# A decoder trunk's MLP: from two token halves to two stages, with a seven-product up projection

## The chip, the cores and the metric
The kernel runs on one core of one Trainium2 chip. The metric is the device time of one execution in microseconds; lower is better. Runs agree to within about 0.3%.

## The reference
One layer of a hybrid decoder for T = 2080 tokens (2048 of a prompt, 32 of eight sample sequences) with model width D = 1024: RMSNorm, one combined projection, three groups of heads (window attention, dilated attention, an RWKV-7 recurrence), an output projection added to the residual, and then the part that is changed, all in float32:
```
x = x + mix @ w_out
u = rmsnorm(x, norm2_g) @ mlp_up            # 1024 -> 4096
x = x + square(relu(u)) @ mlp_down          # 4096 -> 1024
y = rmsnorm(x, final_norm_g)
```

## The kernel before
Every float32 product is made of three passes on TensorE: an operand is split into a rounded high part and a low part (raw minus high), and high x high, high x low and low x high are summed in one PSUM bank (`passes`, L2612 to L2615). ACT makes the high parts by a copy, DVE the low parts by a subtraction.

The stages up to the output projection (projection, attentions, RWKV) aren't touched. `out_project` (L2324) goes over 17 tiles of 128 tokens (one of 32): mixed heads times w_out, DVE adds the residual, ACT and DVE normalise, PE transposes. It takes the second half of the tokens first, whose transposed activations h go to DRAM (`h2T`), then the first half, whose activations stay in SBUF, already split (`keep_high`, `keep_low`).

`mlp` (L2468) then treats the two halves of the tokens one after the other: 1024 tokens as two groups of 512 columns, then 1056 as three of 352. Each half goes over the 32 blocks of 128 hidden features in 16 pairs (`super_loop`, L2457, mostly a hardware loop). For a pair, PE makes the up product (8 blocks of the width x 3 passes for each group, L2639), ACT takes relu and square, DVE repeats the square in full precision and makes the low part; then PE makes the down product of the pair before (L2677): for 8 token tiles and two column halves, 2 features x 3 passes into one of four banks, which DVE adds to the residual rows y in SBUF (L2851, 32 adds in two pairs). Up and down products thus alternate, hidden activations never leave SBUF, and the weights of both products pass once for each half of the tokens. The 32 sample tokens have their down product in plain float32 (L2663), gathered at the end by `collect` (L2649). The final RMSNorm runs per tile behind the last adds (L2748 on ACT, L2828 and L2830 on DVE); that of the first half runs while the second half begins.

All loads and stores are issued by SyncE in one hand-written order, each behind a wait for the buffer it overwrites. Each engine's order is written out by hand too. GpSimd (Pool) does nothing after RWKV; the projection at the start of the kernel has Pool add squares (L378, L382) while DVE splits x (L299). Between two stages there is a barrier of all engines.

## Time and profile before
| | us |
|---|---|
| median of 3 runs | 3247.53 |
| lowest, highest | 3238.03, 3248.34 |
| profiled execution, its span (no other time is given of it) | 3240.8 |
| output projection in that span | about 1551 to 1753 |
| MLP, first and second half of the tokens | about 1753 to 2456, 2456 to 3241 |

The names of tiles in the rows are those of the program, without buffer numbers: `m_hh` and `m_hl` are the split activations, `m_wuh` and `m_wul` the split up weights, `m_uh`, `m_ul`, `m_wdh`, `m_wdl` those of the down product, `m_bank` a PSUM bank. A matmul's record is longer than the distance to the next one, since matmuls overlap in the pipeline; the distance of starts is what a matmul takes of the engine. PEld is the weight load, which runs beside the matmul before.

### The profile page before, as it was taken

How to read it: one execution, taken by the hardware profiler on the slowest of the kernel's cores; microseconds unless marked ns; L12 is line 12 of the kernel's file. 1: busy time of each engine (PE TensorE's matmuls, PEld its weight loads, DVE VectorE, ACT ScalarE, POOL GpSimd, SP SyncE). 2: the span in 40 equal slices, each digit the busy share in tenths (PEclk: the TensorE clock that was granted, in tenths of full speed). 3: DMA queues.
4: the chain of work that ended last, by engine and by line, in shares of the span. 5: the costliest groups of instructions: out<-in, count | busy, mean ns of one | idle time of the engine just before them, and what ended most of it. 6: DMA issues, size and time to landing. Idle time of an engine off the chain costs nothing. (4 is left out here: it accounts for less than half of the span.)

```text
span 3240.8 us, 65672 instructions
## 1 busy us (share of the span) xinstructions
PE 3053.3 (94%) x27080; PEld 2592.6 (80%) x27080; DVE 1562.9 (48%) x3044; ACT 825.3 (25%) x1562; POOL 351.2 (11%) x473
## 2 busy tenths in 40 slices
PE   7999999799788998886999999999999999999998
PEld 6999998466577777785777888888888888888886
DVE  6211121576665666654334444444447445544555
ACT  5000000465423232322234222111224122112212
POOL 4000000454233222310000000000000000000000
PEclk9999999899899999995899999999999999999999
DMA  4121221532222230002454111101124110111111
GB/s 154 70 73 68 72 84 48 139 102 88 88 88 84 96 109 26 22 13 73 152 158 158 52 52 52 52 26 52 52 72 170 52 45 33 52 52 38 40 46 67
DMA packets 135355, 240.45 MB, mean 74 GB/s; under 512 B 21280, under 2 KB 92448, under 8 KB 134624
## 3 DMA queue, kind: packets, MB, share of 16 engines
q1 hardware_dynamic: 135136, 237.29, 21.9%
q8 instruction: 167, 2.74, 0.4%
q14 instruction: 52, 0.43, 0.0%
HBM read 180.92 MB, written 56.33 MB: 73 GB/s over the span
## 5 line engine op out<-in xcount | busy, mean ns | idle before, releaser
L2851 DVE TENSOR_TENSOR m_y<-m_y,m_bank 128x512 f32<-128x512 f32 x512 | 351.3, 687 | 326.1 <-PE m_bank L2615 325.8
L2613 PE MATMUL m_bank<-m_hh,m_wuh 128*128 128x352 f32 (+1 forms) x1280 | 450.0, 352 | 2.4 <-DVE m_hl L2319 2.4
L2615 PE MATMUL m_bank<-m_hh,m_wul 128*128 128x352 f32 (+1 forms) x1280 | 451.0, 352 | 0.0
L2614 PE MATMUL m_bank<-m_hl,m_wuh 128*128 128x352 f32 (+1 forms) x1280 | 450.7, 352 | 0.0
L2613 PE MATMUL m_bank<-m_wdh,m_uh 128*128 128x512 f32 x1024 | 407.9, 398 | 4.8 <-DVE m_wdl L2806 4.7
L2615 PE MATMUL m_bank<-m_wdh,m_ul 128*128 128x512 f32 x1024 | 404.9, 395 | 0.0
L2614 PE MATMUL m_bank<-m_wdl,m_uh 128*128 128x512 f32 x1024 | 403.8, 394 | 0.0
L183 PE MATMUL p_bank<-p_xh,p_wh 128*128 128x416 f32 x800 | 285.3, 357 | 11.1 <-DVE p_wl L304 11.1
L184 PE MATMUL p_bank<-p_xl,p_wh 128*128 128x416 f32 x800 | 282.6, 353 | 0.0
L185 PE MATMUL p_bank<-p_xh,p_wl 128*128 128x416 f32 x800 | 281.8, 352 | 0.0
L2613 PEld LDWEIGHTS m_bank<-m_hh,m_wuh 128*128 128x128 f32 x1280 | 240.6, 188 | 27.0 <-DVE m_hl L2319 2.6
L2614 PEld LDWEIGHTS m_bank<-m_hl,m_wuh 128*128 128x128 f32 x1280 | 241.3, 189 | 24.2
L2615 PEld LDWEIGHTS m_bank<-m_hh,m_wul 128*128 128x128 f32 x1280 | 241.0, 188 | 22.5
L2613 PEld LDWEIGHTS m_bank<-m_wdh,m_uh 128*128 128x128 f32 x1024 | 193.2, 189 | 63.7 <-issue 19.4
L2819 DVE TENSOR_TENSOR m_sq<-m_r 128x352 f32<-128x352 f32 (+1 forms) x160 | 94.4, 590 | 299.5 <-ACT m_r L2716 299.5
L2615 PEld LDWEIGHTS m_bank<-m_wdh,m_ul 128*128 128x128 f32 x1024 | 193.1, 189 | 46.0
L2614 PEld LDWEIGHTS m_bank<-m_wdl,m_uh 128*128 128x128 f32 x1024 | 193.9, 189 | 44.7
L2741 ACT ACTIVATE m_wdh<-m_wdr 128x1024 fp32r<-128x1024 f32 x62 | 62.3, 1053 | 630.7 <-PE m_bank L2615 630.7
L2716 ACT ACTIVATE m_r<-m_bank 128x352 f32<-128x352 f32 (+1 forms) x160 | 83.1, 519 | 456.9 <-PE m_bank L2615 445.6
L359 DVE TENSOR_TENSOR p_ob<-p_bank,p_rs 128x416 f32<-128x416 f32 x70 | 41.4, 592 | 254.4 <-PE p_bank L185 254.4
L183 PEld LDWEIGHTS p_bank<-p_xh,p_wh 128*128 128x128 f32 x800 | 152.7, 191 | 13.5 <-DVE p_wl L304 11.4
L185 PEld LDWEIGHTS p_bank<-p_xh,p_wl 128*128 128x128 f32 x800 | 151.3, 189 | 2.1
(401 smaller groups left out, 5019.5 us busy)
## 6 DMA issues: line engine op xcount, KB each, us to landing
m_wur<-w_up SPq DMA_DIRECT2D x64, 512.0 KB, 6.0
m_wdr<-w_dn SPq DMA_DIRECT2D x64, 512.0 KB, 4.1
p_ring<-units SPq DMA_DIRECT2D x30, 768.0 KB, 6.6
out_projT<-p_ob SPq DMA_DIRECT2D x100, 208.0 KB, 1.9
cp_z<-out_projT SPq DMA_DIRECT2D x8, 1408.0 KB, 7.9
p_wr<-w_fm SPq DMA_DIRECT2D x20, 512.0 KB, 3.6
p_mix<-mixT SPq DMA_DIRECT2D x16, 512.0 KB, 5.1
m_y<-x SPq DMA_DIRECT2D x16, 512.0 KB, 8.1
```

What stands on the lines that cost most here:

```text
L183: pe.matmul(out, wh_, mh, start=(k == 0), stop=False)
L184: pe.matmul(out, wh_, ml, start=False, stop=False)
L185: return pe.matmul(out, wl_, mh, start=False, stop=(k == KC - 1))
L359: dve.tensor_tensor(ob[gi][:, 0:TG], bank[gi][:, 0:TG], rs[:, cols(gi)], ALU.mult).then_inc(evac, 1)
L2613: pe.matmul(out, wh, mh, start=first, stop=False)
L2614: pe.matmul(out, wh, ml, start=False, stop=False)
L2615: return pe.matmul(out, wl, mh, start=False, stop=last)
L2716: act.activation(r[:, q, 0:n], ub[g][:, 0:n], ACT.Relu).then_inc(relued, 1)
L2741: act.activation(wdh[:, j], wdr[:, j], ACT.Copy).then_inc(wd_high, 1)
L2819: dve.tensor_tensor(sq[:, q, 0:n], r[:, q, 0:n], r[:, q, 0:n], ALU.mult).then_inc(u_sq, 1)
L2851: dve.tensor_tensor(yh, yh, db[(2 * a + h) % ND][:, :], ALU.add).then_inc(y_added, 1)
```

## The change
The MLP becomes two stages. The **up stage** takes all tokens in three chunks (696, 696 and 688 tokens), each as two column blocks of 348 or 344. For every chunk it goes over 16 pairs of feature blocks; one pair with one chunk is a unit (48 units, `q`). In a unit the weights are 2 x 2 blocks A (two halves of the width, two feature blocks) and the activations 2 x 2 blocks B (two halves of the width, two token blocks). The four block results come from seven products in place of eight (Winograd's form): of A11, A12, A22 and four sums S1 to S4 of weight blocks with B11, B21, B22 and four sums T1 to T4 of activation blocks. A product is 4 x 3 matmuls of 348 columns.
- Pool makes S1 to S4 for each unit (`sums`, four operations of 128x512), T1 to T4 for each chunk (`mix`, 128x1392 each; for the first chunk `first_mix`, 128x348, inside `out_project`), and two of the seven joins of results (`cross`).
- ACT makes the high parts: of three weight blocks (128x1536) and of the four sums (128x2048), and copies products P1 and P5 out of PSUM (`snap`). At a chunk's end it makes the high parts of the next chunk's seven slots (`high_h`).
- DVE makes the low parts, five joins that read PSUM, and relu times itself on 128x696 twice a unit, and at a chunk's end the low parts of the seven slots (`low_h`). The low part of a slot lies where its raw sum lay, so T2's and T3's wait for the sums that read them.
- The results go to DRAM (`uT`), 1.4 MB a unit; the split activations of a chunk have one buffer, which the next chunk's overwrite product by product.

The **down stage** takes all 16 token tiles for each of 16 pairs of feature blocks, with six banks in place of four, and loads the hidden activations from `uT` (1 MB for 8 tiles and a pair) and splits them there. The rows of y lie where the up stage had its activations, so they are loaded when it has ended. All tiles are normalised in the last pass.

`out_project` takes the tiles in their order, stores every tile's h to DRAM, and in tiles 9 to 12 loads, mixes and splits the first chunk. The buffer of the mixed heads' raw value also takes its low part. Weights arrive in a new order made on the host. There are no hardware loops left in the MLP: it is written out. Up weights pass three times (50 MB), down weights once (17 MB), in place of twice each.

The core of the diff (the new `mlp`; all lines are new but those without a sign):
```
+CHUNKS = [(0, 348), (696, 348), (1392, 344)]
+NC = 348
+KH = KC // 2
+FFB = 32
+FP = FFB // 2
+NUP = len(CHUNKS) * FP
+B11, B21, B22, T1, T2, T3, T4 = range(7)
+A11, A12, A22, S1, S2, S3, S4 = range(7)
+PRODUCTS = [(A11, B11), (S3, T3), (S2, T2), (A12, B21), (S1, T1), (A22, T4), (S4, B22)]
+P1, P7, P6, P2, P5, P4, P3 = range(7)
+NJ = 5
+NPR = len(PRODUCTS)
+PART = KH * NC
...
+        keep = lambda q, i, n, m=1: stage[:, (q % 2 * 4 + i) * NC:(q % 2 * 4 + i + m) * NC].rearrange("p (i t) -> p i t", i=m)[:, :, 0:n]
+        put = lambda q, n: ub[:, q % 2 * 4 * NC:q % 2 * 4 * NC + 4 * n].rearrange("p (f h t) -> p f h t", f=2, h=2)
+        fresh_done = lambda c: 3 * KH + NPR * (c - 1)
...
+            def load_wu(q):
+                if q >= 3:
+                    sp.wait_ge(p_done, NPR * (q - 2))
+                sp.dma_start(wa[q % 3][0][:, :], w_up[q % FP]).then_inc(wu_in[q % 3], 16)
...
+            sp.wait_ge(p_done, NPR * (NUP - 2))
+            load_u(1)
+            sp.wait_ge(p_done, NPR * (NUP - 1))
+            load_u(2)
+            sp.dma_start(wdr[1], w_dn[2:4].rearrange("f p d -> p f d")).then_inc(wd_in[1], 16)
+            store_u(NUP - 1)
+            sp.wait_ge(p_done, NPR * NUP)
             for a in range(NT):
+                sp.dma_start(y[a], x2[P * a:P * a + P, :]).then_inc(y_in[a], 16)
+                if a == 3:
+                    for j in range(2):
+                        sp.dma_start(ut[j], uT[2 * j:2 * j + 2, :, SEQ:T].rearrange("f p t -> p f t")).then_inc(ut_in[j], 16)
+                    sp.wait_ge(zeroed, 1)
+                    for h in range(2):
+                        sp.dma_start(yt[64 * h:64 * h + NS, :], x2[SEQ:T, h * 512:(h + 1) * 512]).then_inc(tail_in, 16)
+            load_u(3)
+            sp.dma_start(fgb, fg).then_inc(fg_in, 16)
...
+            def wait_read(pe, q, p):
+                if p in (P1, P5):
+                    pe.wait_ge(kept, 2 * q + (1 if p == P1 else 2))
+                else:
+                    pe.wait_ge(joined, NJ * q + {P6: 1, P7: 2, P2: 3, P4: 4, P3: 5}[p])
+
+            def product(q, p):
+                c, i = divmod(q, FP)
+                n = CHUNKS[c][1]
+                wj, hj = PRODUCTS[p]
+                if p == 0:
+                    pe.wait_ge(w_low, 2 * q + 1)
+                    if q == 0:
+                        pe.wait_ge(hand.h_low, fresh_done(1))
+                if p == 1:
+                    pe.wait_ge(w_low, 2 * q + 2)
+                if q == 0 and p == 4:
+                    pe.wait_ge(hand.added, hand.NT)
+                if NPR * q + p >= len(ring):
+                    wait_read(pe, *divmod(NPR * q + p - len(ring), NPR))
+                if c and i == 0:
+                    pe.wait_ge(hand.h_low, fresh_done(c) + p + 1)
+                out = pbank(q, p, n)
+                for k in range(KH):
+                    mm = passes(pe, out, w_hi(q, wj)[:, k, :], w_lo(q, wj)[:, k, :],
+                                hand.slot(hh, hj, n)[:, k, :], hand.slot(hl, hj, n)[:, k, :],
+                                k == 0, k == KH - 1)
+                mm.then_inc(p_done, 1)
...
+                    for f in range(2):
+                        mm = passes(pe, db[b % ND][:, :], uh[e % 3][:, f, ts], ul[e % 4][:, f, ts],
+                                    wdh[j % 2][:, f, cols], wdl[j % 2][:, f, cols], f == 0, f == 1)
+                    mm.then_inc(d_done, 1)
...
+            def high_a(q):
+                act.wait_ge(wu_in[q % 3], 16 * (q // 3 + 1))
+                if q >= 2:
+                    act.wait_ge(p_done, NPR * (q - 1))
+                act.activation(wslot(wh[q % 2], A11, 3), wslot(wa[q % 3][0], 1, 3), ACT.Copy).then_inc(w_high, 1)
+
+            def high_s(q):
+                act.wait_ge(summed, 4 * (q + 1))
+                act.activation(wslot(wh[q % 2], S1, 4), ws[q % 2][0][:, :], ACT.Copy).then_inc(w_high, 1)
+
+            def high_h(c, i):
+                j = ORDER[i]
+                n = CHUNKS[c][1]
+                act.wait_ge(p_done, NPR * (FP * c - 1) + i + 1)
+                if j in MIXED:
+                    act.wait_ge(hand.mixed, 4 * (KH + c - 1) + MIXED[j])
+                else:
+                    act.wait_ge(h_in, 32 * c)
+                act.activation(hand.slot(hh, j, n), raw_of(c, j), ACT.Copy).then_inc(hand.h_high, 1)
+
+            def snap(q, p):
+                n = CHUNKS[q // FP][1]
+                act.wait_ge(p_done, NPR * q + p + 1)
+                if q >= 2 and p == P1:
+                    act.wait_ge(u_set, 2 * (q - 1))
+                act.activation(keep(q, 0 if p == P1 else 3, n)[:, 0, :], pbank(q, p, n), ACT.Copy).then_inc(kept, 1)
...
+            for q in range(NUP):
+                edge = (q + 1) // FP if (q + 1) % FP == 0 and q + 1 < NUP else 0
+                begun = q // FP if q % FP == 0 else 0
+                if q + 1 < NUP:
+                    high_a(q + 1)
+                snap(q, P1)
+                if begun:
+                    high_h(begun, 5)
+                    high_h(begun, 6)
+                if edge:
+                    high_h(edge, 0)
+                if q + 1 < NUP:
+                    high_s(q + 1)
+                if edge:
+                    high_h(edge, 1)
+                snap(q, P5)
+                if edge:
+                    for i in (2, 3, 4):
+                        high_h(edge, i)
+                if q == NUP - 6:
+                    high_wd(0)
+                if q == NUP - 5:
+                    high_ut(0)
...
+            def low_a(q):
+                dve.wait_ge(w_high, 2 * q + 1)
+                dve.wait_ge(summed, 4 * (q + 1))
+                raw, low = (wslot(of, 1, 3) for of in wa[q % 3])
+                dve.tensor_tensor(low, raw, wslot(wh[q % 2], A11, 3).bitcast(F32), ALU.subtract).then_inc(w_low, 1)
+
+            def low_s(q):
+                dve.wait_ge(w_high, 2 * q + 2)
+                raw, low = ws[q % 2]
+                dve.tensor_tensor(low[:, :], raw[:, :], wslot(wh[q % 2], S1, 4).bitcast(F32), ALU.subtract).then_inc(w_low, 1)
+
+            def low_h(c, i):
+                j = ORDER[i]
+                n = CHUNKS[c][1]
+                dve.wait_ge(hand.h_high, fresh_done(c) + i + 1)
+                if j in (T3, T2):
+                    dve.wait_ge(hand.mixed, 4 * (KH + c - 1) + (2 if j == T3 else 4))
+                dve.tensor_tensor(hand.slot(hl, j, n), raw_of(c, j), hand.slot(hh, j, n).bitcast(F32),
+                                  ALU.subtract).then_inc(hand.h_low, 1)
...
+            def join(q, to, of, p):
+                n = CHUNKS[q // FP][1]
+                dve.tensor_tensor(keep(q, to, n)[:, 0, :], keep(q, of, n)[:, 0, :],
+                                  pbank(q, p, n), ALU.add).then_inc(joined, 1)
+
+            def relu_square(q, f):
+                n = CHUNKS[q // FP][1]
+                both = keep(q, 2 * f, n, 2)
+                dve.scalar_tensor_tensor(out=put(q, n)[:, f, :, :], in0=both, scalar=0.0, in1=both,
+                                         op0=ALU.max, op1=ALU.mult).then_inc(u_set, 1)
+
+            def join_first(q):
+                dve.wait_ge(p_done, NPR * q + P6 + 1)
+                dve.wait_ge(kept, 2 * q + 1)
+                join(q, 1, 0, P6)
+                dve.wait_ge(joined, NJ * q + 1)
+                join(q, 2, 1, P7)
+                dve.wait_ge(p_done, NPR * q + P2 + 1)
+                join(q, 0, 0, P2)
+
+            def join_rest(q):
+                dve.wait_ge(crossed, 2 * q + 2)
+                dve.wait_ge(p_done, NPR * q + P4 + 1)
+                join(q, 2, 2, P4)
+                if q >= 2:
+                    dve.wait_ge(u_stored[q % 2], 16 * (q // 2))
+                dve.wait_ge(joined, NJ * q + 4)
+                relu_square(q, 1)
+                dve.wait_ge(p_done, NPR * q + P3 + 1)
+                join(q, 1, 1, P3)
+                dve.wait_ge(joined, NJ * q + 5)
+                relu_square(q, 0)
...
+            for q in range(NUP):
+                edge = (q + 1) // FP if (q + 1) % FP == 0 and q + 1 < NUP else 0
+                begun = q // FP if q % FP == 0 else 0
+                if q + 1 < NUP:
+                    low_a(q + 1)
+                if q == 0:
+                    hand.copy_out(dve, hand.NT - 1)
+                if begun:
+                    low_h(begun, 5)
+                    low_h(begun, 6)
+                if edge:
+                    low_h(edge, 0)
+                join_first(q)
+                if q + 1 < NUP:
+                    low_s(q + 1)
+                if edge:
+                    low_h(edge, 1)
+                join_rest(q)
+                if edge:
+                    for i in (2, 3, 4):
+                        low_h(edge, i)
+                if q == NUP - 6:
+                    low_wd(0)
+                if q == NUP - 5:
+                    low_ut(0)
...
+            def sums(q):
+                a21, a11, a12, a22 = (wslot(wa[q % 3][0], i) for i in range(4))
+                s1, s2, s3, s4 = (wslot(ws[q % 2][0], i) for i in range(4))
+                pool.wait_ge(wu_in[q % 3], 16 * (q // 3 + 1))
+                if q >= 2:
+                    pool.wait_ge(p_done, NPR * (q - 1))
+                pool.tensor_tensor(s1, a21, a22, ALU.add).then_inc(summed, 1)
+                pool.tensor_tensor(s3, a11, a21, ALU.subtract).then_inc(summed, 1)
+                pool.wait_ge(summed, 4 * q + 1)
+                pool.tensor_tensor(s2, s1, a11, ALU.subtract).then_inc(summed, 1)
+                pool.wait_ge(summed, 4 * q + 3)
+                pool.tensor_tensor(s4, a12, s2, ALU.subtract).then_inc(summed, 1)
+
+            def mix(c):
+                n, f = CHUNKS[c][1], fresh(c)
+                t = lambda j: hand.slot(hand.mix, j, n)
+                free = lambda i: pool.wait_ge(p_done, NPR * (FP * c - 1) + i + 1)
+                at = 4 * (KH + c - 1)
+                pool.wait_ge(h_in, 32 * c)
+                free(1)
+                pool.tensor_tensor(t(T3), f["b22"], f["b12"], ALU.subtract).then_inc(hand.mixed, 1)
+                free(2)
+                pool.wait_ge(hand.mixed, at + 1)
+                pool.tensor_tensor(t(T2), t(T3), f["b11"], ALU.add).then_inc(hand.mixed, 1)
+                free(4)
+                pool.tensor_tensor(t(T1), f["b12"], f["b11"], ALU.subtract).then_inc(hand.mixed, 1)
+                cross(FP * c - 1)
+                free(5)
+                pool.wait_ge(hand.mixed, at + 2)
+                pool.tensor_tensor(t(T4), f["b21"], t(T2), ALU.subtract).then_inc(hand.mixed, 1)
+
+            def join_kept(q, to, of):
+                n = CHUNKS[q // FP][1]
+                pool.tensor_tensor(keep(q, to, n)[:, 0, :], keep(q, of, n)[:, 0, :],
+                                   keep(q, 3, n)[:, 0, :], ALU.add).then_inc(crossed, 1)
+
+            def cross(q):
+                pool.wait_ge(kept, 2 * q + 2)
+                pool.wait_ge(joined, NJ * q + 2)
+                join_kept(q, 1, 1)
+                pool.wait_ge(crossed, 2 * q + 1)
+                join_kept(q, 3, 2)
+
+            sums(0)
+            for q in range(NUP):
+                if q + 1 < NUP:
+                    sums(q + 1)
+                if (q + 1) % FP == 0 and q + 1 < NUP:
+                    mix((q + 1) // FP)
+                else:
+                    cross(q)
```
The down product's `passes`, its adds and `normalise` are as before but for names and counts. On ACT and DVE the down weights and activations of a pass are split during the pass before (DVE behind tiles 3, 8 and 12).

## Rows read from the trace of the kernel before
**Rows 1.** The page: busy time of the engines; the chain that ended last, by line.
```profile
PE 3053.3 (94%) x27080; PEld 2592.6 (80%) x27080; DVE 1562.9 (48%) x3044; ACT 825.3 (25%) x1562; POOL 351.2 (11%) x473
...
PE m_bank L2613 15%; PE m_bank L2615 15%; PE m_bank L2614 15%; PE m_bank L2663 0%; DVE m_y L2830 0%; DVE m_wdl L2806 0%; DVE m_hl L2319 0%; DVE m_y L2851 0%; ACT m_hh L2298 0%; PE m_bank L2649 0%; DVE m_hr L2307 0%; DVE m_hl L2797 0%; ACT m_hr L2285 0%; ACT m_hr L2291 0%; PE m_bank L2277 0%
```
**Rows 2.** Windows in each half of the MLP: us; busy and count; clock; DMA share; GB/s.
```profile
1858.00:1903.00 45.00, 45.00 (x195) 36.39 (x194) 21.19 (x29) 8.84 (x12) 0.00 (x0) 1.00 0.15 48
...
2903.00:2950.00 47.00, 47.00 (x251) 41.61 (x251) 22.78 (x35) 9.69 (x16) 0.00 (x0) 1.00 0.13 48
```
**Rows 3.** Timeline of PE: first matmul of an up product, and what follows its last.
```profile
2140.22 0.40 PE L2613 MATMUL m_bank<-m_hh,m_wuh 128*128 128x512 f32 x1
...
2162.62 0.39 PE L2613 MATMUL m_bank<-m_wdh,m_uh 128*128 128x512 f32 x1
...
2597.16 0.33 PE L2613 MATMUL m_bank<-m_hh,m_wuh 128*128 128x352 f32 x1
...
2620.32 0.64 PE L2663 MATMUL m_bank<-m_wdr,m_ut 128*32 128x512 f32 x4
```
**Rows 4.** Timeline of PE at the seams of the MLP, and a window (columns of rows 2).
```profile
1752.81 0.39 PE L2385 MATMUL m_bank<-p_wh,p_ml 128*128 128x512 f32 x1
...
1769.26 0.39 PE L2614 MATMUL m_bank<-m_hl,m_wuh 128*128 128x512 f32 x1
...
1766.00:1769.00 3.00, 3.00 (x8) 2.30 (x7) 2.81 (x5) 0.50 (x1) 0.00 (x0) 0.50 1.02 410
...
2456.09 0.76 PE L2613 MATMUL m_bank<-m_wdh,m_uh 128*128 128x512 f32 x1 [3.17 <-DVE m_wdl L2806]
...
3201.92 1.06 PE L2663 MATMUL m_bank<-m_wdr,m_ut 128*32 128x512 f32 x8
...
3230.54 0.40 PE L2615 MATMUL m_bank<-m_wdh,m_ul 128*128 128x512 f32 x1
```
**Rows 5.** Timeline of POOL: two-operand adds of the projection, then subtractions of RWKV.
```profile
33.41 2.00 POOL L378 TENSOR_TENSOR p_xs<-p_xs 128x832 f32<-128x832 f32 x1 [6.79 <-ACT p_xs L262]
35.50 1.08 POOL L382 TENSOR_TENSOR p_rs<-p_xs 128x416 f32<-128x416 f32 x1
36.54 2.29 POOL L378 TENSOR_TENSOR p_xs<-p_xs 128x832 f32<-128x832 f32 x1
38.91 1.29 POOL L382 TENSOR_TENSOR p_part<-p_xs 128x416 f32<-128x416 f32 x1
...
869.04 4.88 POOL L1929 TENSOR_TENSOR cp_zs<-cp_z 128x2816 f32<-128x2816 f32 x1 [12.11 <-DVE rw_rko L2043]
...
1487.38 0.77 POOL L1929 TENSOR_TENSOR cs_zs<-cs_z 128x352 f32<-128x352 f32 x1 [52.31 <-DVE cs_z L1732]
```
**Rows 6.** Groups by line and shape, from 1500 us on; then the waits' line.
```profile
L2851 DVE TENSOR_TENSOR m_y<-m_y,m_bank 128x512 f32<-128x512 f32 x512 | 351.3, 687 | 326.1 <-PE m_bank L2615 325.8
...
L2801 DVE TENSOR_TENSOR m_wul<-m_wur,m_wuh 128x1024 fp32r<-128x1024 f32 x63 | 76.9, 1221 | 10.3 <-ACT m_wuh L2706 10.3
...
L2706 ACT ACTIVATE m_wuh<-m_wur 128x1024 fp32r<-128x1024 f32 x63 | 65.8, 1045 | 3.0 <-DMA m_wur<-w_up 3.0
...
L2716 ACT ACTIVATE m_r<-m_bank 128x352 f32<-128x352 f32 x96 | 44.7, 465 | 227.5 <-PE m_bank L2615 221.5 <-DVE m_sq L2819 4.0 <-issue 1.9
...
L2830 DVE SCALAR_TENSOR_TENSOR m_y<-m_y,m_stat,m_fg 128x1024 f32<-128x1024 f32 x8 | 10.3, 1284 | 0.3
...
PEld m_bank L2613 <- issue: 19.4, 18, 3.6
```
**Rows 7.** DVE in the projection: timeline; one line's durations (ns, min/median/max).
```profile
35.68 5.53 DVE L299 SCALAR_TENSOR_TENSOR p_xl<-p_xs,p_g,p_xh 128x416 fp32r<-128x416 f32 x4
...
L299 DVE SCALAR_TENSOR_TENSOR p_xl<-p_xs,p_g,p_xh x40: 637/646/2370, 6.9 to 57.2; 128x416 fp32r<-128x416 f32 x40
```
**Rows 8.** A window (columns of rows 2) and SyncE's timeline, as the y tiles load.
```profile
1760.00:1763.00 3.00, 1.46 (x10) 0.86 (x8) 0.98 (x4) 0.77 (x4) 0.00 (x0) 1.00 1.03 422
...
1755.26 4.73 SPq L2561 DMA_DIRECT2D m_y<-x  x7
```

More of the change, by code:

```diff
@@ L37, in sb, with twin @@
         return self.ctx.enter_context(self.nc.sbuf_tensor(name, shape, dt, side=self.side))
+    def twin(self, raw, name, shape):
+        with ExitStack() as only:
+            before = only.enter_context(self.nc.sbuf_tensor(raw, shape, F32, side=self.side))
+        return before, self.sb(name, shape, F32R)
     def ps(self, name, shape):
@@ L2167, in out_tiles @@
 def out_tiles():
[L2169 to L2170 removed]
+    return [(P * i, P) for i in range(SEQ // P)] + [(SEQ, NS)]
 class OutWeights:
@@ new lines, in mlp @@
+        fgb = wx[0][:, UN:UN + D]
+        sq = wx[1][:, UN:UN + D]
+        yt = wx[0][:, UN + D:UN + D + 512]
+        ut = [stage[:, i * 2 * NS:(i + 1) * 2 * NS].rearrange("p (f t) -> p f t", f=2) for i in range(2)]
+        pick = stage[:, 4 * NS:6 * NS].rearrange("p (h t) -> p h t", h=2)
+        square_to = stage[:, 6 * NS:6 * NS + D]
+        y = [hand.y_low[:, a * D:(a + 1) * D] for a in range(9)] + [hand.mix[:, a * D:(a + 1) * D] for a in range(NT - 9)]
+        ring = [hand.bank[i] for i in (2, 3, 6, 7, 0, 1)]
@@ L2528, in mlp @@
         normed = s.sem(n_("normed"))
-        out_st = [s.sem(n_(f"out_st{i}")) for i in range(NT)]
-        tail_st = s.sem(n_("tail_st"))
+        out_st = s.sem(n_("out_st"))
         block = ctx.enter_context(nc.Block())
-        first, second = halves
-        width = lambda H: sum(n for _, n in H.groups)
-        finals = [0, 1, 2, 3, NT, 4, 5, 6, 7]
-        ys = lambda a: sq[0:NS].rearrange("p a b -> p (a b)") if a == NT else y[:, a, :]
-        rows = lambda a: NS if a == NT else P
+        wslot = lambda of, i, k0=1: of[:, i * KH * P:(i + k0) * KH * P]
@@ L2608, in _ @@
-            sp.wait_ge(tail_st, 16)
-            for a in range(NT):
-                sp.wait_ge(out_st[a], 32)
-        def passes(pe, out, wh, wl, mh, ml, first, last):
-            pe.matmul(out, wh, mh, start=first, stop=False)
-            pe.matmul(out, wh, ml, start=False, stop=False)
-            return pe.matmul(out, wl, mh, start=False, stop=last)
+            def load_wu(q):
+                if q >= 3:
+                    sp.wait_ge(p_done, NPR * (q - 2))
+                sp.dma_start(wa[q % 3][0][:, :], w_up[q % FP]).then_inc(wu_in[q % 3], 16)
@@ L2684, in _ @@
[L2684 to L2693 removed]
+                    mm = pe.matmul(collected[h][0:NS, :], pick[:, h, :], yt[:, :], start=True, stop=True)
@@ new lines, in _ @@
+            hand.turn(pe, hand.NT - 2)
+            for q in range(NUP):
+                for p in range(NPR):
+                    product(q, p)
+                    if q == 0 and p == 3:
+                        hand.turn(pe, hand.NT - 1)
+            pe.wait_ge(hand.h_out, hand.NT)
+            pe.wait_ge(joined, NJ * NUP)
+            for j in range(FP):
+                for a in range(NT):
+                    if a == 8:
+                        tail(j)
+                    down(j, a)
+                    if j == FP - 1 and a == 10:
+                        collect()
@@ L2771, in _ @@
-            super_loop(act, body_first)
-            high_up(second, 0, 1, units(first, NSUP))
-            act.wait_ge(eps_set, 1)
-            for a in range(NT):
-                act.wait_ge(y_added, turns(first, NSUP - 1) + 2 * a + 2)
-                square(a, a)
-            act.wait_ge(squared, NT)
-            act.activation(st[:, 1, 0:NT], st[:, 0, 0:NT], ACT.Sqrt, bias=eps[:, 0:1], scale=1.0 / D).then_inc(rooted, 1)
-            super_loop(act, body_of(second))
+            high_s(0)
```

825 lines of the change are left out of this document (362 added, 463 removed).

## Prediction
> **What bounds the kernel now.** I read the page first. TensorE is busy 94% of the span, and the chain that ended last has three lines of the MLP, 45% of the span between them [rows 1]. Then the stage windows: inside the MLP, PE is busy for all 45 or 47 us of a window at clock 1.00, while DVE has 21 to 23 us, ACT 9, Pool nothing, and the DMA engines 13 to 15% [rows 2]. Then the timeline, for the spacing of the matmuls: a matmul's start-to-start time is its price (its duration overlaps the next one). 96 matmuls of 512 columns start in 22.40 us, 233.3 ns each; 144 of 352 columns in 23.16 us, 160.8 ns [rows 3]. Both are 0.456 to 0.457 ns a column, so nothing is charged per matmul at 352 columns although the weight loads beside them last 188 ns each. The reader is to see a stage in which only the number of columns counts. What isn't columns is small and sits at three seams [rows 4]: 7.6 us at the start of the MLP (from the end of the matmul at 1752.81 to the one at 1769.26, 16.2 us, of which 37 matmuls account for 8.6), 5.7 us between the halves (3.17 idle, then 13 matmuls 0.43 apart instead of 0.23), and 3.7 us in the last pass (28.9 us from the tail at 3201.9 to the last matmul's end at 3230.8, of which 96 matmuls, the tail's 1.0 and a collect of 1.8 account for 25.2). Behind each such idle stretch the spacing doubles for some 3 to 6 us: the granted clock has gone from 2.4 to 1.2 GHz (0.50 in the window behind the first seam) [rows 4].
>
> **The sum.** The profiled execution has a span of 3240.8 us and no other time of its own; the runs' median, 3247.53, is 6.7 above it, and I carry those 6.7 over. 0.3% is 9.7 us, about what a measurement of this kernel can tell from no change.
>
> Up product, before: 32 blocks x 8 x 3 passes over 1024 tokens in 512s (1536 matmuls) and over 1056 in 352s (2304): 1536 x 0.2333 + 2304 x 0.1608 = 728.9 us. After: 48 units x 7 products x 4 x 3 = 4032 matmuls of 348 or 344 columns; at 0.4569 ns a column 2688 x 0.1590 + 1344 x 0.1572 = 638.7. **Minus 90.2.** The down product keeps its 3072 matmuls of 512 columns and its 64 tail matmuls: 0. Its DVE work keeps its 512 adds at 0.687 us; splits of 2048 columns cost what two of 1024 do. Per pass of 16 tiles that is 32 x 0.687 + 3 x 2.3 = 29 us under 45 us of PE, with six banks between them: covered.
>
> Removed seams: the one between the halves, -5.7; the last pass no longer waits for its split weights (they are made during the pass before), -3.7.
>
> Start of the MLP. Pool now makes four 512-column sums before DVE can split the first weights. Pool prices: 128x416 takes 1.08 us and 128x832 2.00, so 2.2 ns a column over 0.16; but 128x352 and 128x2816 take 0.77 and 4.88, 1.67 ns a column over 0.19 [rows 5]. A 512-column sum is then 1.04 to 1.29 us. Four: 4.2 to 5.2; the split of 1536 columns (0.15 + 1.04 ns a column, from 0.687 and 1.221 us [rows 6]) is 1.75; PE starts 6.1 to 7.1 us after the stage does, runs at the low clock (2.7 us more), and turns a tile in between (1.0). That makes 10.8 for 7.6: **+3.2**.
>
> A unit of the up stage. PE needs 84 matmuls, 13.3 us. DVE: splits 1.75 + 2.29, five joins from PSUM at 0.49 (0.687 for 512), two relu-squares of 696 columns at 0.94 (0.646 for 416 [rows 7], 1.284 for 1024): 8.4. ACT: 1.5 + 1.9 + two copies of 0.46: 4.3 [rows 6]. Pool: four sums and two joins of 348: 5.7 to 7.0. Each fits alone. Do Pool and DVE run beside each other? In the projection four DVE operations that take 0.65 each alone took 5.53 us while Pool ran three, ending one per Pool operation, and Pool's own grew from 2.00 to 2.29 and from 1.08 to 1.29 [rows 5, 7]. So they take turns when both read two SBUF operands. I walked the queues of one unit with that: sums end 7.0 us into the unit, first split 8.9, three joins 10.4, second split 13.2, Pool's two joins 13.9, DVE's rest 4.7 us into the next. The next unit's weights are due at 13.3 and 15.2: they are 4.4 and 2.0 us early. **Hidden: 0**, with 2.0 us of cover; if it goes, the second product of each unit is late.
> The Trainium skill, "SBUF — State Buffer", "Who interferes with whom", calls this pair an exclusive lock for a whole instruction; taken to the letter with the recorded durations the same walk gives 14.0 us a unit, a rival below. "GPSIMD Engine Reference", 3.1, has 4497 ns for a 2048-column add, which as an estimate is the dearer of my two Pool prices; by it alone the two seams below would cost 41 and not 35.
>
> Chunk edges (two). The old activations' buffers are overwritten one by one behind the last unit's products. Pool must do unit sums, then four mixes of 1392 columns (2.5 to 3.24 each) with its two joins in front of the last; DVE must split seven slots of 1392 (1.60 each), and its split of T2 waits for T4, the last mix, since it overwrites what T4 reads. Walk at the dearer price, from the last unit's start: sums 7.0, T3 11.9, T2 16.4, T1 21.6, joins 24.8, T4 28.0; low T3 waits for T2 and ends 23.1, low T2 33.4, low T4 41.9. PE wants them at 15.2, 17.1 and 22.8 and is 19 us late after that unit. At the cheaper price: 12.6. If the two engines didn't exclude each other: 2 to 6. I take 16, and 1.5 for the low clock behind two stalls of 7 us, most of it inside the waits: 17.5 x 2 = +35. Behind Pool's mixes stand the next unit's sums; behind DVE's waits its joins, for which PE's ring of six banks has room.
>
> Near the end of the up stage the first down weights and activations are split (2.3 us each in two units): +1.5 (0 to 3). Up to down: PE waits for the last join, 1 us; the residual rows can be loaded only then, behind the last store of 1.4 MB. DMA moved 422 GB/s when asked [rows 8], so a 512 KB tile takes 1.25 us under PE's 2.8 per tile; issuing one costs 0.68 (7 in 4.73 us). The first tile is there some 8 us after the last matmul, the banks last 8.4: +1.5 (1 to 12: at half that rate the next activations below come at 53 us, 12 beyond what the banks cover). The next activations, behind 8.4 MB, arrive at 32 us and are wanted at 37: 0. Projection of the output: 48 matmuls a tile (11 us) over DVE's split 1.2, adds 1.4, copies 2.7 and, in four tiles, activations' split 3.0 [rows 6]; ACT less than before, Pool's mixes beside it: +1 (0 to 4). Traffic grows by 34 MB; a unit needs 2.4 MB in 13.3 us, 180 GB/s of 422: 0. Unrolled code: PE's weight loads now idle 19.4 us for "issue", 18 times [rows 6]; from nothing to as much again; I take 0. Final normalising: DVE's 2.6 us a tile against PE's 2.8, same end: 0.
>
> -90.2 -5.7 -3.7 +3.2 +35 +1.5 +1.5 +1 = -57.4. Span 3183.4, time **3190**.
>
> **Rivals.**
> Faster, 3162: Pool and DVE overlap at the edges after all, or Pool's subtractions go at 1.67 and the order of the queues is kinder. For: the 0.77 and 4.88 us rows are subtractions, and three of four sums are. Against: rows 7. Edges 2 x 4 in place of 35: 27 less. Chance 0.17.
> Lock-bound, 3236: the two engines exclude each other for their whole durations, unit 14.0 (0.7 x 43 = 30), edges 24 + 1.5 each (+16). For: DVE and Pool together hold 11.6 to 12.9 of 13.3 us. Against: in rows 7 Pool lost only 0.2 to 0.3 us per DVE operation of 0.65. Chance 0.22.
> Slower, 3304: the ring between three engines closes. Pool's joins wait for DVE, DVE's rest waits for Pool's joins, and the next sums stand behind them; nothing of one unit overlaps the next: 5.2 + 1.75 + 1.5 + 2.3 + 1.9 + 2.9 = 15.5 us a unit, 2.2 x 45 = 99 more, and 16 at the edges. It decides from 13.3 + 57/48 = 14.5 us a unit. For: cover of only 2.0 us. Against: Pool's sums need only the products of two units before. Chance 0.12.
> No saving in PE: below 352 columns the 188 ns loads could show, 84 x 0.188 = 15.8 us a unit, 120 more. Against: at 352 they are already longer than the 160.8 spacing and cost nothing. Chance 0.02, within the slower ones.
>
> **How the numbers follow.** Forecast 0.49 with its own range 3175 to 3215, faster 0.17, lock-bound 0.22, slower 0.12. The range 3160 to 3246 leaves out the slower rivals and the low end of the faster one. Faster by 9.7 us (below 3237.8): 0.49 + 0.17 + about two thirds of the lock-bound case, 0.14: 0.80. Within 0.3%: 0.08. Slower: 0.12.
>
> **What would show it.** Spacing of 348-column matmuls 0.159 us; units 13.3 us apart with DVE ending its relu-squares some 5 us into the next; waits of PE for the split of activations of 7 and 8 us at units 16 and 32, and nearly none for split weights; DVE's two-operand subtractions longer than their 1.75 and 2.29 us wherever Pool runs; PE whole in the down stage. Units at 14 or more, or PE waiting for weights in every unit, make it wrong on one side; edges under 8 us on the other.

## The result, and the profile after

| | before | changed |
|---|---|---|
| median us (runs) | 3245.50 (4) | 3194.22 (4), 3187.36 to 3206.45 |
| ratio, 95% interval | | 0.9849, 0.9825 to 0.9873 |
| profiled execution: span | 3240.8 | 3185.6 (its own time 3187.36) |
| last matmul of `out_project` starts | 1752.81 | 1750.18 |
| from there to the start of the last matmul of the MLP | 1477.7 | 1424.8 |

The change saves 51 us, 1.5%; 3190 had been forecast. The page, as in [rows 1]:

```profile
PE 2969.4 (93%) x27272; PEld 2581.3 (81%) x27272; DVE 1832.1 (58%) x3068; ACT 827.0 (26%) x1315; POOL 892.6 (28%) x785
...
L3042 POOL TENSOR_TENSOR m_stage<-m_stage 128x348 f32<-128x348 f32 (+1 forms) x96 | 183.4, 1910 | 160.3 <-DVE m_stage L2881 101.9
```
PE has 84 us less, DVE 269 us more and Pool 541 us more. Pool's joins of 348 columns are recorded with 1910 ns each, where Pool operations of that shape take 937 to 959 ns in `out_project`. The recorded duration thus holds time in which Pool stands and waits (e1 shows this).

Windows of the changed kernel, inside a chunk of the up stage, behind the first edge, and as the down stage begins (columns of [rows 2]):
```profile
1858.00:1903.00 45.00, 45.00 (x284) 45.00 (x283) 31.43 (x30) 13.41 (x13) 34.76 (x21) 1.00 0.41 149
...
1985.00:2000.00 15.00, 8.37 (x28) 7.99 (x29) 14.05 (x8) 3.55 (x3) 13.96 (x6) 0.50 0.12 48
...
2447.00:2457.00 10.00, 10.00 (x45) 7.95 (x44) 6.54 (x10) 3.46 (x2) 0.00 (x0) 1.00 1.04 385
```
Inside a chunk PE is whole, with Pool and DVE together recorded for 66 of 45 us. At the edge they are both busy for 14 of 15 us while PE works half the time, at the low clock of 1.2 GHz. The down stage has PE whole although DMA moves 385 GB/s.

The waits of PE in the up stage (us in total, times, longest), then SyncE's timeline: the issue of a weight load marks the end of a unit.
```profile
PE m_bank L2675 <- DVE m_hl L2876: 17.5, 5, 5.4
PE m_bank L2675 <- DVE m_stage L2881: 9.6, 4, 4.8
PE m_bank L2675 <- DVE m_wul L2863: 7.0, 1, 7.0
PE m_bank L2675 <- DVE m_wsl L2868: 2.0, 2, 1.0
PE m_bank L2675 <- issue: 0.8, 1, 0.8
```
```profile
1975.85 0.34 SPq L2590 DMA_DIRECT2D m_wur<-w_up  x1
...
2007.94 0.35 SPq L2590 DMA_DIRECT2D m_wur<-w_up  x1
```
Units inside the first two chunks end 13.38 us apart, in the third 13.23; the two edge units take 32.1 (shown) and 32.6.

One unit inside a chunk, from the timelines of DVE and POOL (the unit before ended at 1842.03, this one at 1855.42):
```profile
1849.15 1.76 DVE L2863 TENSOR_TENSOR m_wul<-m_wur,m_wuh 128x1536 fp32r<-128x1536 f32 x1 [2.63 <-POOL m_wsr L3020]
1850.83 1.49 DVE L2881 TENSOR_TENSOR m_stage<-m_stage,m_bank 128x348 f32<-128x348 f32 x3
1852.23 2.97 DVE L2868 TENSOR_TENSOR m_wsl<-m_wsr,m_wuh 128x2048 fp32r<-128x2048 f32 x1
...
1856.65 1.34 DVE L2887 SCALAR_TENSOR_TENSOR m_u<-m_stage 128x696 f32<-128x696 f32 x1
```
```profile
1852.11 3.89 POOL L3042 TENSOR_TENSOR m_stage<-m_stage 128x348 f32<-128x348 f32 x2 [3.06 <-ACT m_stage L2790]
1855.96 1.28 POOL L3015 TENSOR_TENSOR m_wsr<-m_wur 128x512 f32<-128x512 f32 x1
1857.21 1.94 POOL L3016 TENSOR_TENSOR m_wsr<-m_wur 128x512 f32<-128x512 f32 x1
1859.10 1.93 POOL L3018 TENSOR_TENSOR m_wsr<-m_wsr,m_wur 128x512 f32<-128x512 f32 x1
1861.12 1.30 POOL L3020 TENSOR_TENSOR m_wsr<-m_wur,m_wsr 128x512 f32<-128x512 f32 x1
```
Against its forecast step by step, in us from the unit's start: first split ends 8.9 (8.9 forecast), three joins 10.3 (10.4), second split 13.2 (13.2), Pool's joins 14.0 (13.9). Its sums for the next unit end 7.0 into that (7.0). The wait before Pool's joins in this unit ends with ACT's copy of the fifth product (3.06), so with PE; in the stage 31 of these waits end with DVE's joins and 15 with the copy.

Where the 55.2 us of span went: 2.6 before the MLP (2.3 of it ahead of `out_project`, in stages that weren't touched), 52.9 in the MLP, and 0.4 given back behind its last matmul. In the MLP the start costs 3.7 more than before (from the end of the last projection matmul, 1750.4, to the first unit's end, 1775.1, is 24.7 us for a unit of 13.4, so 11.3 over it, and it was 7.6), the edges 18.7 + 19.35 = 38.1, two late units 2 x 1.95 = 3.9, the passage to the down stage 0.9. What is left, 52.9 + 3.7 + 38.1 + 3.9 + 0.9 = 99.5, is the saving in columns and in the two old seams together; 90.2 + 5.7 + 3.7 = 99.6 had been forecast. The units inside the chunks show the first of the three by itself: 32 x 13.38 + 16 x 13.23 = 639.8 us of up product, where the forecast had 638.7.

### The profile page after: what moved, and what is told of

The parts are those of the page before. It is cut to its first block and busy times, and to the rows that moved or that the text cites. A ratio compares the mean times of both kernels' runs of the same rounds, so it can differ in the third digit from the quotient of the medians.

```text
span 3185.6 us, 64433 instructions
## 1 busy us (share of the span) xinstructions
PE 2969.4 (93%) x27272; PEld 2581.3 (81%) x27272; DVE 1832.1 (58%) x3068; ACT 827.0 (26%) x1315; POOL 892.6 (28%) x785
## 3 DMA queue, kind: packets, MB, share of 16 engines
q1 hardware_dynamic: 164448, 313.84, 29.2%
## 5 line engine op out<-in xcount | busy, mean ns | idle before, releaser
L2675 PE MATMUL m_bank<-m_hh,m_wuh 128*128 128x348 f32 (+1 forms) x1344 | 437.9, 326 | 36.2 <-DVE m_hl L2876 17.5
L2676 PE MATMUL m_bank<-m_hl,m_wuh 128*128 128x348 f32 (+1 forms) x1344 | 436.9, 325 | 0.0
L189 PE MATMUL p_bank<-p_xh,p_wh 128*128 128x416 f32 x800 | 286.2, 358 | 10.1 <-DVE p_wl L310 10.1
L2932 DVE TENSOR_TENSOR m_y_low<-m_y_low,m_bank 128x512 f32<-128x512 f32 x288 | 194.5, 686 | 139.8 <-PE m_bank L2677 135.0
L2677 PE MATMUL m_bank<-m_hh,m_wsl 128*128 128x348 f32 (+1 forms) x768 | 249.5, 325 | 0.0
L3042 POOL TENSOR_TENSOR m_stage<-m_stage 128x348 f32<-128x348 f32 (+1 forms) x96 | 183.4, 1910 | 160.3 <-DVE m_stage L2881 101.9
L2932 DVE TENSOR_TENSOR m_mix<-m_mix,m_bank 128x512 f32<-128x512 f32 x224 | 152.1, 686 | 117.6 <-PE m_bank L2677 116.4
L2677 PE MATMUL m_bank<-m_wuh,m_wul 128*128 128x512 f32 x512 | 200.9, 392 | 0.0
L2677 PE MATMUL m_bank<-m_hh,m_wul 128*128 128x348 f32 (+1 forms) x576 | 186.5, 324 | 0.0
L190 PEld LDWEIGHTS p_bank<-p_xl,p_wh 128*128 128x128 f32 x800 | 151.8, 190 | 1.3 <-issue 0.9
L2677 PEld LDWEIGHTS m_bank<-m_hh,m_wsl 128*128 128x128 f32 x768 | 146.7, 191 | 0.0
```

The costliest lines, as they stand in the source:

```text
L189: pe.matmul(out, wh_, mh, start=(k == 0), stop=False)
L190: pe.matmul(out, wh_, ml, start=False, stop=False)
L2675: pe.matmul(out, wh_, mh, start=first, stop=False)
L2676: pe.matmul(out, wh_, ml, start=False, stop=False)
L2677: return pe.matmul(out, wl_, mh, start=False, stop=last)
L2932: dve.tensor_tensor(yh, yh, db[b % ND][:, :], ALU.add).then_inc(y_added, 1)
```

## Experiments

Stages that no edit touches move by up to 18 us between executions: the first up matmul starts at 1759.1 in the changed kernel's profile and at 1758.6 to 1776.3 in those below. So each run is read by its **up stage**, from the start of the first up matmul to that of the first down matmul, and by its units. For the changed kernel that is 1759.13 to 2444.49, 685.4 us. The expectations of e6 and e8 use 693.1 for it; the differences are the same. e1 to e7 were executed once each, e8 to e10 five times (the median is given); e1 to e4 ran on one chip, e5 to e8 on a second, e9 and e10 on a third.

| run | time | up stage | edge units | other units |
|---|---|---|---|---|
| changed | 3194.2 | 685.4 | 32.1, 32.6 | 13.38 |
| e1 mixes small | 3182.3 | 665.2 | 22.4, 21.7 | 13.38 |
| e2 product twice | 3263.7 | 762.2 | 29.2, 28.9 | 15.29 |
| e3 a sum more | 3254.4 | 743.0 | 37.9, 36.0 | 14.52 |
| e4 two sums more | 3311.4 | 804.5 | 41.5, 40.2 | 15.88 |
| e5 as e3, joins first | 3214.8 | 708.2 | 37.4, 37.0 | 13.38, then 13.73 |
| e6 cross from PSUM | 3194.3 | 680.7 | 32.3, 31.7 | 13.38 |
| e7 mixes on DVE | 3192.4 | 672.9 | 25.9, 25.5 | 13.38 |
| e8 both | 3176.3 | 665.4 | 24.4, 24.3 | 13.38 |
| e9 and T3 ahead | 3172.1 | 663.3 | 23.5, 23.3 | 13.38 |
| e10 changed, again | 3196.1 | 685.4 | 32.1, 32.6 | 13.38 |

"Other units" are those inside the first two chunks.

My theory was that of the prediction: columns bound the stage inside a chunk, and at an edge Pool's sums and DVE's splits, which take turns, do. The rivals were a ring that is as long as PE's work, an edge set by DVE or by loads, and engines that work side by side.

**e1: the activation sums of the later chunks cut away.**
```
-                t = lambda j: hand.slot(hand.mix, j, n)
+                t = lambda j: hand.slot(hand.mix, j, 2)
+                f = {k: b[:, :, 0:2] for k, b in f.items()}
```


> Leaves out the four sums of activation blocks (T1 to T4) for the second and third chunk: Pool's four additions there handle 8 columns of 1392, and the split reads a raw block of the same size instead, so DVE's and ACT's work and all matmuls stay. My theory: the two chunk edges cost 38 us because Pool's four mixes and its exclusion with DVE's splits stand in a row; without them what is left of an edge is DVE's seven splits, and the unit with its edge takes about 21.5 us instead of 32.1 and 32.6: about 21 us less in all, span about 3165. Rival (the splits themselves, seven of 1.6 us and more behind the last unit's products, or the loads of the new activations, set the edge whatever Pool does): an edge unit stays at 30 us or more, span 3180 to 3186. Units inside a chunk stay at 13.4 in both.

Edges of 22.4 and 21.7, the up stage 20.2 us shorter. The splits and the loads stayed, so more than half of what an edge costs comes from Pool's four mixes. What the tiny operations show beside it, in POOL's and DVE's timelines of e1:
```profile
1984.82 0.21 POOL L3030 TENSOR_TENSOR m_mix<-m_rows 128x8 f32<-128x8 f32 x1
1985.17 1.62 POOL L3033 TENSOR_TENSOR m_mix<-m_mix,m_rows 128x8 f32<-128x8 f32 x1
1987.42 0.90 POOL L3035 TENSOR_TENSOR m_mix<-m_rows 128x8 f32<-128x8 f32 x1 [0.63 <-PE m_bank L2677]
```
```profile
1984.96 1.76 DVE L2863 TENSOR_TENSOR m_wul<-m_wur,m_wuh 128x1536 fp32r<-128x1536 f32 x1 [2.63 <-POOL m_wsr L3020]
1986.64 1.61 DVE L2876 TENSOR_TENSOR m_hl<-m_rows,m_hh 128x1392 fp32r<-128x1392 f32 x1
```
Eight columns take 0.21 us alone. The operation issued at 1985.17, behind the begin of a DVE split, ends at 1986.79, that split at 1986.72; the next ends at 1988.32, DVE's at 1988.25. Pool stands until the whole DVE instruction is over.

**e2: twelve matmuls more in each unit.**
```
-                for k in range(KH):
+                for k in [*range(KH)] * (2 if p == 0 else 1):
```


> The first product of each of the 48 units runs its 12 matmuls twice: 12 x 0.159 = 1.91 us more TensorE work a unit, nothing else. If TensorE's columns bound the up stage inside a chunk (my theory), a unit goes from 13.4 to 15.3 us, and because an edge hides behind it only in part, the stage gets about 77 us longer (span about 3263), with edge units at 29 to 30 instead of 32. Rival (the ring of Pool, DVE and ACT is already as long as TensorE's work, with 13.38 us a unit being its period and not TensorE's): a unit stays well under 15.3, at 13.4 to 14.5, and the stage gets at most 50 us longer.

15.29 us a unit and 76.8 in the stage, as the theory had it. PE bounds a unit, and the slack it gives the others is worth 3 us at an edge.

**e3 and e4: one and two Pool sums more in each unit**, ahead of S2 and S4.
```
                 pool.tensor_tensor(s3, a11, a21, ALU.subtract).then_inc(summed, 1)
+                pool.tensor_tensor(s3, a11, a21, ALU.subtract).then_inc(again, 1)
+                pool.wait_ge(again, 1 * q + 1)
```


> One of Pool's four sums of weight blocks (512 columns, 1.27 us alone) is made twice in every unit. This tells how much room is left in the ring of Pool and DVE behind TensorE. My walk, in which Pool and DVE take turns when both read two SBUF operands: the unit stays at 13.4 (the room is just over one sum), the two edges grow by 2.4 us each, the up stage by 5 us in all. Rival A (the engines take turns for their whole durations, so that DVE and Pool already fill 13.3 us): a unit grows by 0.7 to 1.3 us, 30 to 60 us in all. Rival B (they don't hinder each other; Pool has 9.6 us of work in 13.3): unit 13.4, edges up by 1.3 at most, under 3 us in all.

> The same sum three times in every unit, 2.5 us more of Pool. By the walk with turns the ring now closes: unit 14.4 us, edges 39.8, the up stage 58 us longer. Rival A (whole durations exclusive): a unit grows by 2 to 2.6 us, 95 us or more. Rival B (no hindrance; Pool would have 12.1 of 13.3 us and DVE its 8.4): the unit stays at 13.4, the edges grow by 2.5 each, under 8 us in all.

Here my expectation fell: 14.52 and 15.88 us a unit, 57.6 and 119.1 us in the stage; rival A's numbers. Part of it was a slip: my walk had the additional sum behind the four, where nobody waits for it; the kernel has it in front of the sums that DVE's split waits for. With the right place the walk, redone after these results and so no forecast, gives 14.4 and 15.7 us, 54 and 116 in the stage. These two runs therefore can't tell my walk from rival A; e5 does. The trace of e3 shows the loop:
```profile
1865.44 1.29 POOL L3023 TENSOR_TENSOR m_wsr<-m_wur,m_wsr 128x512 f32<-128x512 f32 x1
1869.72 3.87 POOL L3045 TENSOR_TENSOR m_stage<-m_stage 128x348 f32<-128x348 f32 x2 [2.98 <-DVE m_stage L2882]
1873.55 1.29 POOL L3016 TENSOR_TENSOR m_wsr<-m_wur 128x512 f32<-128x512 f32 x1
```
```profile
1866.83 1.76 DVE L2864 TENSOR_TENSOR m_wul<-m_wur,m_wuh 128x1536 fp32r<-128x1536 f32 x1 [3.87 <-POOL m_wsr L3023]
1868.51 1.49 DVE L2882 TENSOR_TENSOR m_stage<-m_stage,m_bank 128x348 f32<-128x348 f32 x3
1869.92 2.88 DVE L2869 TENSOR_TENSOR m_wsl<-m_wsr,m_wuh 128x2048 fp32r<-128x2048 f32 x1
```
The last sum ends at 1866.73; DVE's split starts 0.1 later; behind it stand DVE's joins; Pool's joins wait for those (2.98 us idle), run under DVE's second split (3.87 us for the two, 1.87 alone), and the next unit's sums start only then. A further sum adds 15.88 - 14.52 = 1.36 us, so four sums close this loop in 14.52 - 1.36 = 13.16 us, worked out and not measured. PE needs 13.38. The room was 0.2 us a unit.

**e5: e3's additional sum, with DVE's joins ahead of its split** in all units but those at an edge.
```
+                early = not edge and not begun
+                if early:
+                    join_first(q)
                 if q + 1 < NUP:
                     low_a(q + 1)
...
-                join_first(q)
+                if not early:
+                    join_first(q)
```


> As e3 (one sum of Pool made twice in every unit, where a unit came to 14.52 us), and DVE's first three joins of a unit now stand ahead of its split of the next unit's first weights instead of behind it; in the two edge units and behind them the order stays. Theory 1, a ring of two engines: in e3 Pool's joins waited for DVE's joins, these stood behind DVE's split, the split waited for Pool's sums, and the next sums stood behind Pool's joins. With the joins first the wait of Pool (2.98 us a unit in e3) is gone, the ring is open and a unit is TensorE's 13.4 again; my walk has the up stage 31 us shorter than e3's. Theory 2, capacity: Pool and DVE take turns, their two-operand work with the additional sum fills 14.3 us or more, and in whatever order it stands a unit stays at 14.3 to 14.5.

The same work in another order, and the up stage is 34.7 us shorter (743.0 to 708.2); units two to nine of the first chunk and the first four behind its edge take 13.38, the later ones 13.73. The expectations had 13.4 (order) and 14.3 to 14.5 (capacity): the second is out, the first is met only in part. POOL's timeline of a later unit:
```profile
1869.74 1.28 POOL L3027 TENSOR_TENSOR m_wsr<-m_wur,m_wsr 128x512 f32<-128x512 f32 x1
1873.40 3.71 POOL L3049 TENSOR_TENSOR m_stage<-m_stage 128x348 f32<-128x348 f32 x2 [2.38 <-ACT m_stage L2791]
```
The wait for DVE's joins is gone; a shorter one for ACT's copy of the fifth product has taken its place, since the second split now reaches PE late (PE waits for it in eleven units, 0.2 to 0.3 us each). So most of e3's loss (0.8 of 1.14 us a unit) was the order and not the capacity, and 0.35 us is left with a second, longer way round over PE.

**e6: the fifth product joined by DVE straight from PSUM**, Pool's two joins and ACT's copy left out. In this and the next three the last transposed tile is copied out behind unit 0's work, which moves one weight load by 4 us and no unit behind it.
```
+            def cross(q, to, of, n):
+                dve.wait_ge(p_done, NPR * q + P5 + 1)
+                dve.wait_ge(joined, NJ * q + n)
+                join(q, to, of, P5)
```


> Pool's two joins of 348 columns a unit are taken off Pool and off ACT's copy: DVE adds the fifth product straight from PSUM, two more joins of 0.5 us. Orders otherwise as in the changed kernel, the activation sums stay on Pool. If exclusion holds only where both engines read two SBUF operands, this takes 1.9 us of Pool out of each unit and each edge for 1.0 of DVE that doesn't collide: units stay 13.4 (TensorE), edges 30.0 instead of 32.4, the late unit 13.2 instead of 15.2; the up stage 7 us shorter than the changed kernel's 693.1 us. Rival (DVE's own length sets the edges): edges get 1 us longer each, 33 to 34.

A partial miss. 4.7 us shorter, 7 forecast. The two late units give 3.9 (the walk had one, 2.0); the edges hardly moved (+0.3 and -0.9) where the walk had 2.4 less each and the rival 1 more. Pool's joins at the edge weren't on the path that I had them on: counted from the end of the last unit's products, Pool's last mix now ends 3.6 us earlier in the first edge, but it runs beside DVE's split of T3 (4.53 us, 2.32 in the changed kernel), and the split of T2, for which PE waits, starts 0.2 us later than before.

**e7: the four activation sums of an edge from Pool to DVE**, as T3, T2, T4, T1.
```
+            def mix(c, j):
...
+                dve.tensor_tensor(t(j), a, b, op).then_inc(hand.mixed, 1)
...
+            last = "mT3 jf mT2 l0 l1 mT4 la mT1 j4 ls r1 l2 j3 r0 l3 l4 l5"
```
(`la`, `ls`: splits of the next unit's weights; `jf`, `j4`, `j3`: joins; `r`: relu-squares; `l0` to `l6`: splits of the slots.)

> The four sums of activation blocks at each edge (1392 columns) go from Pool to DVE, as T3, T2, T4, T1, woven among its splits; Pool keeps its weight sums and its joins. At DVE's price a sum is 1.6 us instead of 3.2, and under exclusion it is the sum of both engines' time that counts: edge and following unit together 40.3 us instead of 45.7, the up stage about 11 us shorter. Rival (Pool and DVE work side by side): DVE gets 6.4 us more work on top of its own at an edge, and the edges get 3 to 6 us longer.

12.5 us shorter, 11 forecast. DVE was given 6.4 us more at an edge, beside 20 of its own (8.4 of a unit and seven splits of 1.6), and the edge lost 6 to 7, where the rival of engines side by side had 3 to 6 more. Not all of it need come from the move: the order of DVE's and ACT's work at the edge was changed with it (T4 ahead of T1, the splits of weights behind some of the activations'), and no run has the one without the other. That the engines don't work side by side rests on e1's rows; this run fits it.

**e8: both.**
```
+            last = "l0 mT3 la ls mT2 jf x1 mT4 x3 j4 r1 j3 l1 mT1 r0 l2 l3 l4 l5 l6"
```


> e6 and e7 together, with an order of DVE's work at the edge found with the walk: Pool makes only the four weight sums of a unit. Walk: units 13.4, edges 23.8, following unit 13.8, up stage 18.6 us shorter than the changed kernel's 693.1, so 674.5; the time 3194.2 - 18.6 = 3175.6, ratio to the kernel before 0.9785. Rival (DVE's length sets the edge, no gain from taking Pool's work away): edge and following unit at 44 or more, the up stage at 690 or more.

The up stage is 20.0 us shorter (18.6 forecast); time 3176.3, ratio to the kernel before 0.9799, 95% interval 0.9771 to 0.9826. Pool is recorded for 6.5 us a unit inside a chunk where it was 10.3. PE's waits in its up stage:
```profile
PE m_bank L2675 <- DVE m_hl L2872: 7.8, 2, 4.0
PE m_bank L2675 <- DVE m_wul L2859: 7.0, 1, 7.0
PE m_bank L2675 <- issue: 5.5, 3, 2.4
```
27.1 us of waits for DVE's activation splits and joins have become 7.8 and two of 2.4, one at each edge, that the view puts down to "issue". PE's and DVE's timelines name their cause:
```profile
1987.36 0.63 PE L2675 MATMUL m_bank<-m_hh,m_wuh 128*128 128x348 f32 x1 [2.42 <-issue]
```
```profile
1986.21 1.91 DVE L2877 TENSOR_TENSOR m_stage<-m_stage,m_bank 128x348 f32<-128x348 f32 x4
```
PE's product there goes into the bank that the second of these four joins reads; that join ends at 1987.26 and PE starts 0.1 later, as it does at the other edge. It is the changed kernel's wait for a free bank (4.0 us there), shortened.

**e9: T3 made ahead, in B12's place**, a quarter in each of four units (T1 then as B22 - T2, and DVE's joins ahead of its splits in every unit inside a chunk); and **e10: the changed kernel again**, on the same chip.
```
+                if q < 2 * FP and 6 <= q % FP < 6 + KH:
...
+                    dve.tensor_tensor(f["b12"][:, k, :], f["b22"][:, k, :], f["b12"][:, k, :], ALU.subtract).then_inc(ahead3, 1)
```


> e8, and in addition T3 = B22 - B12 of the next chunk is made ahead, in B12's place, in four pieces of 348 columns in DVE's slack of four units, so that only T2, T1 (as B22 - T2) and T4 are left for the edge. If the two-operand work of DVE behind the last unit's products is what an edge costs now, one sum less and an earlier T2 give edges of 22.1 instead of 24.4 and the up stage 3 us less than e8's 665.4: 662. Rival (what is left of the edge is TensorE's own restart: its low clock and idle time for instructions, 5.5 us in e8): edges stay at 24, the up stage at 665. Against the changed kernel on the same chip 20 to 23 us less, 0.6 to 0.7%.

> The changed kernel itself, unedited, timed again beside e9 on one chip, so that the two can be told apart directly. Up stage (first up matmul to first down matmul) 685.4 us as in its first profile, edge units 32.1 and 32.6; its other stages move by some us from run to run, so the time is 3187 to 3206.

e10 repeats the up stage of the changed kernel to 0.1 us. e9's edges lie between the two theories, 23.4, the up stage 2.1 us under e8's. Its time is 3172.1 (3167.3 to 3174.8) against e10's 3196.1 (3194.7 to 3199.7) beside it, 0.75% less; ratio to the kernel before 0.9765, 0.9746 to 0.9785. It has the shortest up stage here; its time can't be told from e8's, since the runs overlap and the chips differ. What each edge still costs is 10.1 us. In the first it is 8.7 us of stalls, ahead of the first product (the bank, as in e8) and of the third (T2's split), and 1.2 in 9 matmuls that start 0.29 us apart instead of 0.16; in the second 6.9 and 2.8. No run goes further.

## Why the prediction was right

By its steps, in us:

| term | forecast | measured |
|---|---|---|
| columns, middle seam, last pass | -90.2 -5.7 -3.7 | -99.5 together |
| start of the MLP | +3.2 | +3.7 |
| two edges | +35 | +38.1 |
| late units | +1.5 | +3.9 |
| into the down stage | +1.5 | +0.9 |
| output projection | +1 | -0.3 |
| stages before it | 0 | -2.3 |
| behind the last matmul | 0 | +0.4 |
| span | -57.4 | -55.2 |

The columns did what was said: units of 13.38 (e2 shows that PE sets them, at 0.159 us a matmul) and no charge for weight loads. The down stage's cover held. The dearer Pool price, taken from the projection's rows [rows 5], holds for subtractions too: the first mix of an edge takes 3.21 us for 1392 columns and 3.16 for 1376, which is 2.2 ns a column over 0.16. The rival that had subtractions at 1.67 is out.

That the span came within 2.2 us is in part luck. The terms of the MLP sum to -52.9 for a forecast of -58.4; the stages before it took 2.6 less than in the profile before, where 1 more had been forecast, and they move by more than that between executions.

**The step that was wrong** cost nothing here: "Hidden: 0, with 2.0 us of cover". The walk itself was right to 0.1 us at each point, but the 2.0 us is how early a split is, and that isn't room, by which I mean how much longer the loop of waits may get before it is longer than PE's work. The same numbers close a loop: sums 0.6 to 7.0 (6.4), split to 8.9 (1.9), joins to 10.4 (1.5), Pool's joins to 13.9 (3.5), and then the next sums. That is 13.3 us, the unit itself. e3 and e4 put the room at 0.2 us, and 1.3 us of additional work a unit outside PE made the up stage 58 us longer. The lead of 2 us only delays the loss: in e3 units two and three take 13.38, the fifth and those behind it 14.52. The slower rival was the right mechanism, taken with a joint of its loop in the wrong place (it had nothing overlap, 15.5 us). At 0.12 it had too little. In the changed kernel itself the loop doesn't decide: at 13.16 it is just shorter than PE's 13.38.

**The lock.** I held against the lock-bound rival that Pool lost only 0.2 to 0.3 us per DVE operation [rows 7]. e1's rows show that Pool does wait for the whole of a DVE instruction; e7 and e8 came out as the sum of both engines' work has it. The Trainium skill, "SBUF — State Buffer", "Who interferes with whom", has it so: the pair is an exclusive lock for a whole instruction, and a DVE operation with one SBUF and one PSUM operand isn't in it. This case's rows agree with the second half as well: the joins that read PSUM take 497 to 520 ns in all 240 instances, with Pool busy beside them (142) or not (98). The rival's 14.0 us came from queueing the recorded durations end to end; Pool's 1.29 us and the 0.87 of DVE's relu-square side by side give 1.94, so some 0.2 us of a pair do overlap, and with the joins free the loop is 13.16.

**The edges** came out at the right size (38.1 for 35) with a first stall that I didn't have. The walk of the queues held here too, counted from the last unit's start at 1962.5: Pool's last mix ends 27.6 us in (28.0 forecast), the splits of T3, T2 and T4 at 23.7, 32.8 and 41.2 (23.1, 33.4, 41.9). PE waits first for a free bank, 4.0 us for DVE's joins (`m_stage` in the waits), which stand behind two splits that took 4.68 and 4.55 us for 1.75 and 1.60 alone:
```profile
1969.62 4.68 DVE L2863 TENSOR_TENSOR m_wul<-m_wur,m_wuh 128x1536 fp32r<-128x1536 f32 x1 [2.62 <-POOL m_wsr L3020]
1974.22 4.55 DVE L2876 TENSOR_TENSOR m_hl<-m_rows,m_hh 128x1392 fp32r<-128x1392 f32 x1
1978.69 1.48 DVE L2881 TENSOR_TENSOR m_stage<-m_stage,m_bank 128x348 f32<-128x348 f32 x3
1980.09 3.86 DVE L2868 TENSOR_TENSOR m_wsl<-m_wsr,m_wuh 128x2048 fp32r<-128x2048 f32 x1
```
```profile
1969.47 3.21 POOL L3029 TENSOR_TENSOR m_mix<-m_rows 128x1392 f32<-128x1392 f32 x1
1972.82 4.48 POOL L3032 TENSOR_TENSOR m_mix<-m_mix,m_rows 128x1392 f32<-128x1392 f32 x1
1977.27 4.54 POOL L3034 TENSOR_TENSOR m_mix<-m_rows 128x1392 f32<-128x1392 f32 x1
```
"PE's ring of six banks has room" was therefore wrong at the edge. The two waits for the activations' splits are 3.6 and 5.3, not 7 and 8: with the 4.0 ahead of them 12.9 us for 15. What makes up for it is the clock, for which I had 1.5 us an edge. In the first edge 33 matmuls start 0.29 us apart instead of 0.16, in a stretch with a granted clock of 0.50 (the window above), and cost 4.3 us; the three stalls, by the starts of the matmuls around them, take nearly all of the other 14.4.

**The late units** were under-priced: two splits of 2048 columns in a loop with 0.2 us of room cost 1.95 each. With Pool's joins gone (e6, e8) they cost nothing. **The 6.7 us** between span and median that I carried over were spread between runs: the profiled execution of the changed kernel took 1.8 us more than its span. It was the shortest of its four executions, so the span, missed by 2.2, flatters the forecast; the time was missed by 4.2.

## What to carry to other kernels

Close every loop of queues between engines and compare its period with that of the engine which bounds: how early an operand is ready says nothing about that. Where GpSimd and VectorE both read two SBUF operands, add their times instead of comparing each with the bound; an operation moved from the slower to the faster of the two then paid here even on the busier engine (e7, with the order changed too); moving it to a PSUM operand paid in the late units and not at the edges (e6). Judge an edit by its stage, since stages that it doesn't touch can move by more than it brings.
